# Gate products of a PEER block with bf16 one-hots and the gate in three bf16 parts, on one Trainium2 core

## What is computed

```python
N_KEYS = 128; N_EXPERTS = N_KEYS * N_KEYS; PEER_HEADS = 8; PEER_TOPK = 16
# per token and head: the 16 best of 16384 experts, by the sum of two key scores
cidx = i1[..., :, None] * N_KEYS + i2[..., None, :]
top_s, pos = lax.top_k(cand, PEER_TOPK)
idx = jnp.take_along_axis(cidx, pos, axis=-1)
gate = jax.nn.softmax(top_s, axis=-1)
# per token: 8 * 16 = 128 slots
u = jnp.take(expert_u, ib, axis=0)
a = jnp.einsum('tkd,td->tk', u, hb)
w = gb * jax.nn.gelu(a, approximate=False)
vsel = jnp.take(expert_v, ib, axis=0)
out = jnp.einsum('tk,tkd->td', w, vsel)
```

## Time and profile before

| | us |
|---|---|
| median of three runs | 1858.34 (1857.7 to 1862.29) |
| the profiled execution | 1853.51 |
| its span, first to last instruction | 1851.8 |
| TensorE busy (MATMUL) in the span | 1755.0 (95%) |
| TensorE weight loads | 1456.2 (79%) |
| VectorE busy | 1174.9 (63%) |
| ScalarE busy | 712.6 (38%) |
| GpSimd busy | 612.4 (33%) |
| gate stage, first tile to last product | 664.1 to 1011.9 |

### The profile page before, as it was taken

How to read it: one execution, slowest core, us unless ns; L and a number is a source line. 1 busy time by engine, 2 the same in 40 slices (tenths; PEclk the granted TensorE clock), 3 DMA queues, 4 the chain that set the end, 5 groups by cost and what they waited for, 6 DMA issues and landing times. The chain is left out here.

```text
span 1851.8 us, 23150 instructions
## 1 busy us (share of the span) xinstructions
PE 1755.0 (95%) x8253; PEld 1456.2 (79%) x8253; DVE 1174.9 (63%) x2055; ACT 712.6 (38%) x1133; POOL 612.4 (33%) x471
## 2 busy tenths in 40 slices
PE   6999896969999999999998999999799999999997
PEld 5888575758877788888887888888588888888886
DVE  5766596549999945454453333332378787778877
ACT  5213355443322355555554232222333333333333
POOL 1000000205667632222221000000556677667750
PEclk8999788989999999999999999999899999999999
DMA  9563000422244334656556655554678999889986
GB/s 375 190 236 114 1 1 1 182 114 71 67 136 141 134 138 155 193 164 193 180 177 205 231 173 185 187 187 152 239 279 311 342 326 348 312 326 335 340 321 229
DMA packets 160413, 369.94 MB, mean 200 GB/s; under 512 B 16608, under 2 KB 78560, under 8 KB 157024
## 3 DMA queue, kind: packets, MB, share of 16 engines
q1 hardware_dynamic: 137824, 302.08, 47.0%
q0 software_dynamic: 22528, 67.19, 10.2%
HBM read 306.30 MB, written 62.91 MB: 199 GB/s over the span
## 5 line engine op out<-in xcount | busy, mean ns | idle before, releaser
L2208 PE MATMUL bank<-hl,actT 128*128 128x512 f32 x2304 | 524.4, 390 | 13.4 <-DVE actT L2143 13.4
L2208 PEld LDWEIGHTS bank<-hl,actT 128*128 128x128 f32 x2304 | 433.2, 188 | 104.6 <-DVE hl L2138 14.6
L1921 PE MATMUL bank<-actT,hl 128*128 128x512 f32 x1248 | 285.3, 391 | 7.2 <-DVE hl L1892 7.0
L1921 PEld LDWEIGHTS bank<-actT,hl 128*128 128x128 f32 x1248 | 235.5, 189 | 56.8 <-DVE hl L1892 7.2
L1775 PE MATMUL bank<-actT,hl 128*128 128x512 f32 x1152 | 273.6, 393 | 1.8 <-PEq L1315 1.8
L1556 PE MATMUL bank<-actT,hl 128*128 128x512 f32 x1056 | 249.1, 395 | 15.4 <-PEq L1057 10.4
L1775 PEld LDWEIGHTS bank<-actT,hl 128*128 128x128 f32 x1152 | 212.8, 188 | 44.0 <-issue 2.2
L1556 PEld LDWEIGHTS bank<-actT,hl 128*128 128x128 f32 x1056 | 197.5, 189 | 60.2 <-DVE hl L194 10.8
L2096 ACT ACTIVATE hl<-v_raw 128x1024 fp32r<-128x1024 f32 x128 | 135.6, 1060 | 273.3 <-PE bank L2208 237.0
L2138 DVE TENSOR_TENSOR hl<-v_raw,hl 128x1024 fp32r<-128x1024 f32 x128 | 156.8, 1225 | 82.4 <-ACT hl L2096 68.9
L2055 POOL DMA_INDIRECT rows<-in_v,own_index x65 | 83.4, 1283 | 378.8 <-POOLq L1815 308.1
(11 more groups left out here) (253 smaller groups left out, 2167.7 us busy)
## 6 DMA issues: line engine op xcount, KB each, us to landing
raw<-in_u SPq DMA_DIRECT2D x128, 512.0 KB, 3.7
v_raw<-in_v SPq DMA_DIRECT2D x128, 512.0 KB
expert_gates<-gates SPq DMA_DIRECT2D x12, 2048.0 KB, 9.8
group_gates<-expert_gates SPq DMA_DIRECT2D x32, 768.0 KB
wada<-in_w_ada SPq DMA_DIRECT2D x10, 2048.0 KB, 8.6
acts_in<-early_activations SPq DMA_DIRECT2D x100, 192.0 KB
early_activations<-kept_acts SPq DMA_DIRECT2D x52, 256.0 KB, 2.1
early_activations<-gate_acts SPq DMA_DIRECT2D x48, 256.0 KB, 2.3
```

Source lines behind the costliest of these rows:

```text
L1921: last = nc.tensor.matmul(m.psum[u % 2][:], hl[:, x, u % m.split, kc * P:(kc + 1) * P], m.actT[:, z, kc, :], start=(kc == 0 and j == 0), s ...
L2208: last = nc.tensor.matmul(bank(t, half)[:], w[:, x, j, t * P:(t + 1) * P], v[:, z, j, half * S:(half + 1) * S], start=(first and j == 0 an ...
```

## The change

The one-hots of both keys are made in bf16, in the layout of `hits`, and both are operands of the product as they are, without a copy to float32: `first[:, b, :, u]` is the stationary operand and takes every eighth element. The gate is split once, ahead of the rounds, into three bf16 parts whose sum is the float32 gate; each round VectorE multiplies the second one-hot by each part (`scaled`), and each token's product becomes three bf16 matmuls that accumulate in PSUM. GpSimd has no program in this stage any more, ScalarE scales nothing and evicts both banks, and VectorE evicts none. The core of the diff:

```diff
-ACT_ROWS = 4
+PARTS = 3
...
-        first_bf = sb("first_bf", [P, SD], BF16)
-        hits = sb("first_hits", [P, BUFS, NKEY, ROUND], BF16)
-        onehot1 = sb("onehot1", [P, BUFS, ROUND, NKEY])
-        onehot2 = sb("onehot2", [P, BUFS, ROUND, NKEY])
+        keys_bf = sb("keys_bf", [P, 2, SD], BF16)
+        part = sb("gate_part", [P, PARTS, SD], BF16)
+        left = sb("gate_left", [P, 2, SD])
+        first = sb("first_hits", [P, BUFS, NKEY, ROUND], BF16)
+        second = sb("second_hits", [P, NKEY, ROUND], BF16)
+        scaled = sb("second_scaled", [P, BUFS, PARTS, NKEY, ROUND], BF16)
...
-        @block.gpsimd
-        def _(pool):
...
-                    nc.gpsimd.tensor_tensor(
-                        onehot1[:, b % BUFS, 0:pool_n, :].rearrange("p t k -> p k t"), hits[:, b % BUFS, :, 0:pool_n],
-                        slotsT[:, 2, n].unsqueeze(1).to_broadcast([P, NKEY, pool_n]), ALU.mult
-                        ).then_inc(pool_rows, 1)
...
-            def scale_rows(r):
...
-                act.wait_ge(gated, r * CHUNKS + 1)
-                at = r % per_half * ROUND
-                A(gates[:, k, :, at:at + PER], chunk_bank(r, 0)[:].rearrange("p (t j) -> p j t", t=PER), ACT.Copy
-                  ).then_inc(gates_read[0], 1)
+                for c in range(CHUNKS):
+                    act.wait_ge(gated, r * CHUNKS + c + 1)
+                    at = r % per_half * ROUND + c * PER
+                    A(gates[:, k, :, at:at + PER], chunk_bank(r, c)[:].rearrange("p (t j) -> p j t", t=PER), ACT.Copy
+                      ).then_inc(gates_read, 1)
...
-            m.dve.then(dve, V.tensor_copy(first_bf[:], slotsT[:, 0, :]))
+            V.tensor_copy(keys_bf[:], slotsT[:, 0:2, :])
+            m.dve.then(dve, V.tensor_copy(part[:, 0, :], slotsT[:, 2, :]))
+            m.dve.then(dve, V.tensor_tensor(left[:, 0, :], slotsT[:, 2, :], part[:, 0, :], ALU.subtract))
+            m.dve.then(dve, V.tensor_copy(part[:, 1, :], left[:, 0, :]))
+            m.dve.then(dve, V.tensor_tensor(left[:, 1, :], left[:, 0, :], part[:, 1, :], ALU.subtract))
+            m.dve.then(dve, V.tensor_copy(part[:, 2, :], left[:, 1, :]))
...
-                V.tensor_tensor(onehot2[:, r % BUFS], iota.unsqueeze(1).to_broadcast([P, ROUND, NKEY]),
-                                slotsT[:, 1, n].unsqueeze(2).to_broadcast([P, ROUND, NKEY]), ALU.is_equal
-                                ).then_inc(second_ready, 1)
...
+                m.dve.then(dve, V.tensor_tensor(second[:], iota_bf, keys_bf[:, 1, n].unsqueeze(1).to_broadcast(over_keys),
+                                                ALU.is_equal))
+                V.tensor_tensor(first[:, r % BUFS], iota_bf, keys_bf[:, 0, n].unsqueeze(1).to_broadcast(over_keys),
+                                ALU.is_equal).then_inc(first_ready, 1)
+                for p in range(PARTS):
+                    V.tensor_tensor(scaled[:, r % BUFS, p], second[:], part[:, p, n].unsqueeze(1).to_broadcast(over_keys),
+                                    ALU.mult).then_inc(scaled_ready, 1)
+                dve.wait_ge(scaled_ready, (r + 1) * PARTS)
...
-                if n >= 1:
-                    read_second_half(n - 1)
-            read_second_half(count - 1)
...
+                pe.wait_ge(first_ready, i * per_half + (b + 1))
+                pe.wait_ge(scaled_ready, i * (per_half * PARTS) + (b + 1) * PARTS)
...
-                        last = nc.tensor.matmul(chunk_bank(b, c)[:, k * NKEY:(k + 1) * NKEY],
-                                                onehot1[:, b % BUFS, u, :], onehot2[:, b % BUFS, u, :],
-                                                start=True, stop=True)
+                        for p in range(PARTS):
+                            last = nc.tensor.matmul(chunk_bank(b, c)[:, k * NKEY:(k + 1) * NKEY],
+                                                    first[:, b % BUFS, :, u], scaled[:, b % BUFS, p, :, u],
+                                                    start=(p == 0), stop=(p == PARTS - 1))
```

More of the change, by code:

```diff
@@ L1619, in stage_gates @@
         slotsT, raw, hl = m.slotsT, m.raw, m.hl
-        iota, iota_bf = m.iota, m.iota_bf
+        iota_bf = m.iota_bf
         gates = sb("gates", [P, 2, NKEY, TB])
-        first_bf = sb("first_bf", [P, SD], BF16)
-        hits = sb("first_hits", [P, BUFS, NKEY, ROUND], BF16)
-        onehot1 = sb("onehot1", [P, BUFS, ROUND, NKEY])
-        onehot2 = sb("onehot2", [P, BUFS, ROUND, NKEY])
+        keys_bf = sb("keys_bf", [P, 2, SD], BF16)
[4 more added lines that the diff above has]
+        scaled = sb("second_scaled", [P, BUFS, PARTS, NKEY, ROUND], BF16)
         acts = sb("gate_acts", [P, RAW, S])
         sem = m.sem
-        hits_ready, second_ready = sem("hits_ready"), sem("second_ready")
-        pool_rows, act_rows = sem("pool_rows"), sem("act_rows")
+        first_ready, scaled_ready = sem("first_ready"), sem("scaled_ready")
         gated = sem("gated")
-        gates_read = [sem("gates_read_by_act"), sem("gates_read_by_dve")]
+        gates_read = sem("gates_read")
         acts_stored = m.acts_stored = [sem(f"acts_stored{i}") for i in range(RAW)]
@@ L1637, in stage_gates @@
         per_half = TB // ROUND
-        pool_n = ROUND - ACT_ROWS
         block = own.enter_context(nc.Block())
@@ L1651, in store_gates @@
                 p, k = divmod(q, 2)
-                for c in range(CHUNKS):
-                    sp.wait_ge(gates_read[c], (q + 1) * per_half)
+                sp.wait_ge(gates_read, (q + 1) * per_half * CHUNKS)
                 dst = a.gates[:, 0:NKEY * SD].rearrange("p (g n) -> p g n", n=NTB * JG * TB)
@@ L1666, in _ @@
                 sp.wait_ge(acts_stored[u], 16 * count // RAW)
-        @block.gpsimd
-        def _(pool):
[L1670 to L1676, removed]
-                    nc.gpsimd.tensor_tensor(
-                        onehot1[:, b % BUFS, 0:pool_n, :].rearrange("p t k -> p k t"), hits[:, b % BUFS, :, 0:pool_n],
-                        slotsT[:, 2, n].unsqueeze(1).to_broadcast([P, NKEY, pool_n]), ALU.mult
-                        ).then_inc(pool_rows, 1)
-            body(0, True)
-            with pool.Fori(1, rounds // per_half) as i:
-                body(i, False)
         @block.scalar
@@ L1742, in onehots @@
                 n = slice(r * ROUND, (r + 1) * ROUND)
-                V.tensor_tensor(hits[:, r % BUFS], iota_bf,
-                                first_bf[:, n].unsqueeze(1).to_broadcast([P, NKEY, ROUND]), ALU.is_equal
-                                ).then_inc(hits_ready, 1)
-                V.tensor_tensor(onehot2[:, r % BUFS], iota.unsqueeze(1).to_broadcast([P, ROUND, NKEY]),
-                                slotsT[:, 1, n].unsqueeze(2).to_broadcast([P, ROUND, NKEY]), ALU.is_equal
-                                ).then_inc(second_ready, 1)
[L1750 to L1757, removed]
+                over_keys = [P, NKEY, ROUND]
+                m.dve.then(dve, V.tensor_tensor(second[:], iota_bf, keys_bf[:, 1, n].unsqueeze(1).to_broadcast(over_keys),
[6 more added lines that the diff above has]
+                dve.wait_ge(scaled_ready, (r + 1) * PARTS)
             for n in range(count):
@@ L1778, in tile, with round_ @@
                 last.then_inc(m.unit_used, 1)
-            def round_(i, b, first):
-                pe.wait_ge(pool_rows, i * per_half + (b + 1))
-                pe.wait_ge(second_ready, i * per_half + (b + 1))
+            def round_(i, b, first_body):
+                pe.wait_ge(first_ready, i * per_half + (b + 1))
+                pe.wait_ge(scaled_ready, i * (per_half * PARTS) + (b + 1) * PARTS)
                 for c in range(CHUNKS):
[L1784 to L1788, removed]
+                    if not (first_body and b < BUFS):
+                        pe.wait_ge(gates_read, i * (per_half * CHUNKS) + (b - BUFS) * CHUNKS + c + 1)
                     for k in range(PER):
                         u = c * PER + k
-                        last = nc.tensor.matmul(chunk_bank(b, c)[:, k * NKEY:(k + 1) * NKEY],
-                                                onehot1[:, b % BUFS, u, :], onehot2[:, b % BUFS, u, :],
-                                                start=True, stop=True)
+                        for p in range(PARTS):
+                            last = nc.tensor.matmul(chunk_bank(b, c)[:, k * NKEY:(k + 1) * NKEY],
+                                                    first[:, b % BUFS, :, u], scaled[:, b % BUFS, p, :, u],
+                                                    start=(p == 0), stop=(p == PARTS - 1))
                     last.then_inc(gated, 1)
```

1 line of the change is left out of this document (removed).

## The result

The changed kernel takes 2137.6 us (median of 4 runs, 2134.2 to 2140.3) against 1858.0 us before: 1.149 times, 95% interval 1.147 to 1.152, 280 us slower. The forecast had the sign, and the range (1835 to 1921) missed the size by far: it had +44 us. The profiled execution has a span of 2135.0 us, 283.2 more than before.

What follows compares the result with a forecast made beforehand. TensorE's own instructions were taken to bound the gate stage. Slower bf16 pairs (+42.6 us), transitions (+0.6) and the start (+0.5) summed to +43.7 us on 1858.3, giving 1902 us, range 1835 to 1921.

Steps and rivals of the forecast that it cites:

- the sign: Whole kernel: the change makes it slower, +43.7 us in sum; chance of slower 0.62.
- What bounds the kernel: Gate stage: it lasts as long as TensorE's own instructions, so work taken from GpSimd and ScalarE is worth zero.
- The break-even of 75 ns a pair: Gate products: 24 bf16 pairs replace products costing 1.80 us a round, so the change gains only below 75 ns each.
- the lower bound of 56: Gate products: one bf16 pass of 128 columns takes 56 ns, taken as half of a 112 ns float32 pair.
- I take the ratio, 112 ns: Gate products: the 16-byte step doubles a bf16 pair's 56 ns, as it about doubles ScalarE's time per element; +42.6 us.
- the three readings of ScalarE's row: ScalarE's read at a 16-byte step, carried to a TensorE pair: ratio 112 ns, added time 142 to 181, element pace 232.
- the term 24p: Gate products of a round: 24 bf16 pairs at p each, beside 5.44 us of tile; at 112 ns a round is 8.13 us.
- Rival 4: Gate products: ScalarE's time per element carries over, 142 to 232 ns a pair, +77 to +181 us, 1936 to 2040; chance 0.19.
- The weights: Gate products: stationary operand, read at a 16-byte step like the moving one; the step got no separate price.
- Going between the kinds of tile: TensorE, float32 tiles to bf16 products and back: may expose a load, 0 to 4.6 us over 48 rounds; 0.6 taken.
- VectorE, ScalarE, the start: Gate stage: VectorE 4.4 us a round, ScalarE 2.6 to 2.9, both hidden; longer preparation at the start +0.5 us once.
- The 81 ns: Gate products: the skill's settled step for load-and-multiply pairs of 128 columns; with that alone an estimated +7 us.

## Why the prediction was wrong, by its own steps

- **What bounds the kernel**: right. TensorE had no wait in the stage before and has one of 0.5 us after, so the work taken from GpSimd and ScalarE could bring nothing.
- **The break-even of 75 ns a pair** and the lower bound of 56: right. In order a pair takes 56 ns, and the kernel is faster than before.
- **The step that failed** is "I take the ratio, 112 ns". A pair took 234 ns. Of the three readings of ScalarE's row the last gave the size: an element no faster than 1.8 ns. The ratio took the 56 ns of a pair in order for the time of its reading, but 16 lines at 1.8 ns are 29 ns and are hidden behind the columns, while 128 lines are 234 and are not. The step is the term 24p, mis-sized by 234 - 112 = 122 ns x 1152 = 141 us. TensorE's 1.77 to 1.83 ns per line lies at the upper end of what the earlier trace rows left for ScalarE, 0.83 + 0.7 to 1.0, and it is the same at TensorE's two clocks; that the memory holds both engines to one pace is suggested by this and not shown.
- **Rival 4 was argued away by a misread row.** "TensorE reads float32 columns far faster than ScalarE reads its elements" compared elements; four float32 elements in order share a line, and 512 in 227 ns are 128 lines at 1.77 ns, the same pace. That row could not speak against the rival. Rival 4 with p = 232 gave 2040 us.
- **A term was missing**: the clock. The prediction took the granted 1.00 as given and asked of each cost only what it adds; slow pairs in a row brought the clock to 0.78 and the tiles from 5.44 to 7.3 us a round, 90 us. With both, 1858 + 183 + 90 + 2 for the changes between the kinds + 0.5 = 2134. Of the 4 us that are left of 2138, the stages ahead can hold most: the gate stage starts 3.1 us later in the changed kernel's profile (667.2 us) than in that of before.
- **The weights** were feared as much as the moving operand; their step costs 6 to 7 ns a pair, 8 us in all. Going between the kinds of tile was put at 0.6 us in sum; in order it is 0.1 us a round, 5 us, and with slow pairs 0.05, 2 us.
- **VectorE, ScalarE, the start**: VectorE's operations of a round run from 809.99 to 814.48, 4.5 us where 4.4 was said; ScalarE has 17.23 / 84 x 13.0 = 2.7 us a round; TensorE waited 0.53 us for the first `scaled` where 0.5 was said.
- **The Trainium skill**: the rule on lines of 16 bytes (SBUF — State Buffer, section "Door 1: The DMA port swizzle") is borne out as to the size of a line: 117 ns at a step of 8 bytes, 227 to 234 at 16 and 232 at 32. The trace disagrees with the same section of the Trainium skill where that has two accesses to a line suffice for full speed and counts steps of up to 8 bf16 as free: two bf16 to a line took 117 ns in place of 56, and the step of 8 bf16 took 234. The 81 ns of the Trainium skill's TensorE: Matmul & The Clock Gate, section "Back-to-back issue gap", is not what this stream of pairs does: 56 ns.

## What to carry to other kernels

Lay out what TensorE streams so that neighbouring columns are neighbouring elements, and count lines of 16 bytes, not elements, to price it: here 1.8 ns for each, wherever that is more than the columns take. If VectorE wants another order for its bf16 rate, duplicate the small operand in pairs rather than let TensorE read with a step. And when an engine-bound stage gets instructions that stretch without computing more, price the clock too: TensorE was busy all the time here, and a third of the growth (90 of 276 us) was its clock.

## What the runs showed of the hardware

- The moving operand costs 1.77 to 1.83 ns per line of 16 bytes, at 2.4 and at 1.2 GHz alike: 117 ns for 128 bf16 at 8 bytes, 227 to 234 at 16, 232 at 32, 227 for float32 at 16. In order, 128 bf16 take 56 ns, so it shows only where it is longer than the columns.
- Weights are far less sensitive: a step of 16 bytes lengthens their load from 98 to 147 ns and a pair from 56 to 62.
- The granted clock fell to 0.93, 0.88 and 0.78 with 12, 16 and 24 bf16 matmuls of 234 ns in a row and stayed at 1.00 with 8, and with 24 spread out, TensorE being busy without a pause in each. It also stayed at 1.00 with 16 float32 matmuls of 227 ns in a row and with 24 bf16 ones of 117 ns. What in these stretches the clock goes by was not settled.
